# Experts, projection and solution of a two-block transformer in one block, with two norms behind the experts as one step

## The reference

```python
# first block, end: product-key experts, then the norm that closes the block
h2 = rmsnorm(x, g_ffn)
x = x + peer_ffn(h2, w_peer_q, sub_keys, u_tab, v_tab)
x = rmsnorm(x, g_final)
# second block, start: norm, gated delta rule in both directions
h = rmsnorm_2(x, norm_mix[0])
x = x + gated_deltanet_bidir(h, ...)   # projection, conv, decays, triangular solution, w_out
x = x + squared_relu_mlp(rmsnorm_2(x, norm_mlp[0]), w1, w2)
# then a dilated window attention with its own norm, a second mlp, a last norm
def rmsnorm(x, g):
    return x * rsqrt(mean(x * x) + 1e-6) * g
```

## Time and profile before

| | us |
|---|---|
| time, median of 3 runs | 1988.34 (1986.02 to 1992.40) |
| profiled execution, device time | 1990.63 |
| profiled execution, span of the trace | 1988.5 |
| TensorE busy in the span | 1880.9 (95%) |
| VectorE busy | 1289.9 (65%) |
| ScalarE busy | 898.8 (45%) |
| mean granted TensorE clock | 0.972 of 2.4 GHz |

### The profile page before, as it was taken

One profiled execution on the slowest core, in us unless ns is written; L12 is line 12 of the kernel. 1 busy time (PEld: TensorE's weight loads), 2 busy tenths in 40 slices (PEclk: granted clock), 3 DMA queues, 4 the chain that ended last, 5 costly groups with the idle time before them and its releaser, 6 DMA issues. The chain is left out here.

```text
span 1988.5 us, 31375 instructions
## 1 busy us (share of the span) xinstructions
PE 1880.9 (95%) x13035; PEld 1741.9 (88%) x13035; DVE 1289.9 (65%) x2034; ACT 898.8 (45%) x1161; POOL 18.1 (1%) x24
## 2 busy tenths in 40 slices
PE   7999998999999999999999969888899999999997
PEld 7998897899999999888888859778799889789985
DVE  5656874798788888655555557885466455446633
ACT  6457532343443433444444446666255343435532
POOL 0000000000000000000000000000000001000000
PEclk9999999999999999999999979987899999999999
DMA  6443354444444444455555533310254456525443
GB/s 225 171 172 132 123 191 152 146 174 171 157 146 153 147 152 146 179 209 190 191 191 196 196 127 129 126 44 23 77 178 169 186 198 210 131 74 191 177 183 117
DMA packets 44741, 310.66 MB, mean 156 GB/s; under 512 B 5166, under 2 KB 5678, under 8 KB 8144
## 3 DMA queue, kind: packets, MB, share of 16 engines
q1 hardware_dynamic: 42576, 303.58, 42.3%
q0 software_dynamic: 1472, 4.86, 1.5%
q10 hardware_dynamic: 576, 0.55, 0.1%
HBM read 306.84 MB, written 2.13 MB: 155 GB/s over the span
## 5 line engine op out<-in xcount | busy, mean ns | idle before, releaser
L310 DVE TENSOR_TENSOR s_ring_lo<-s_ring,s_w_hi 128x2048 fp32r<-128x2048 f32 x236 | 540.6, 2291 | 253.1 <-ACT s_w_hi L304 248.6
L304 ACT ACTIVATE s_w_hi<-s_ring 128x2048 fp32r<-128x2048 f32 x235 | 448.1, 1907 | 157.3 <-PE bank L347 77.9
L347 PE MATMUL bank<-s_hT_hi,s_w_hi 128*128 128x256 f32 x2016 | 292.8, 288 | 4.3 <-PEq L455 2.4
L347 PE MATMUL bank<-s_hT_hi,s_ring_lo 128*128 128x256 f32 x2016 | 285.4, 285 | 1.0 <-DVE s_ring_lo L310 0.8
L347 PEld LDWEIGHTS bank<-s_hT_hi,s_w_hi 128*128 128x128 f32 x2016 | 263.2, 194 | 9.5 <-issue 8.1
L347 PEld LDWEIGHTS bank<-s_hT_hi,s_ring_lo 128*128 128x128 f32 x2016 | 262.2, 194 | 1.8 <-DVE s_ring_lo L310 1.8
L1544 PE MATMUL bank<-s_w_hi,s_hT_lo 128*128 128x512 f32 x1024 | 242.6, 389 | 0.3 <-issue 0.3
L1544 PEld LDWEIGHTS bank<-s_w_hi,s_hT_lo 128*128 128x128 f32 x1024 | 192.1, 188 | 40.3 <-issue 0.4
L347 PE MATMUL bank<-s_hT_lo,s_w_hi 128*128 128x256 f32 x1056 | 152.2, 288 | 0.0
L347 PEld LDWEIGHTS bank<-s_hT_lo,s_w_hi 128*128 128x128 f32 x1056 | 140.3, 197 | 0.0
L347 PE MATMUL bank<-s_x_r,s_w_hi 128*128 128x256 f32 x960 | 134.8, 283 | 0.0
(11 more groups left out here) (413 smaller groups left out, 2413.6 us busy)
## 6 DMA issues: line engine op xcount, KB each, us to landing
s_ring<-weights SPq DMA_DIRECT2D x282, 1024.0 KB, 4.8
s_arena<-bias_by_distance POOLq DMA_DIRECT2D x12, 384.0 KB, 7.4
s_arena<-mem SPq DMA_DIRECT2D x1, 1024.0 KB, 6.0
s_x<-x SPq DMA_DIRECT2D x1, 1024.0 KB, 13.6
x_away<-s_x SPq DMA_DIRECT2D x1, 1024.0 KB, 4.8
s_arena<-sub_keys SPq DMA_DIRECT2D x1, 1024.0 KB, 6.9
s_arena<-x_away SPq DMA_DIRECT2D x1, 1024.0 KB, 6.8
out<-s_x SPq DMA_DIRECT2D x1, 1024.0 KB, 4.0
```

The lines of the kernel that those rows point to most:

```text
L304: act.activation(k.w_hi[:, u % 2, :], k.ring[:, u % RING, :], ACT.Copy).then_inc(k.hi_ready, 1)
L310: dve.tensor_tensor(k.ring_lo[:, u % RING, :], k.ring[:, u % RING, :], plain(k.w_hi[:, u % 2, :]), ALU.subtract).then_inc(k.lo_ready, 1)
L347: last = pe.matmul(out[:, nb * S:(nb + 1) * S], w[:, c, nb * P:(nb + 1) * P], h[:, c, :], start=(n == 0 and c == 0), stop=(n == 2 and c == 7))
```

## The change

- The first two blocks' semaphores are allocated by hand and cleared ahead of the norm before the experts, instead of those of the experts and the projection being cleared behind these.
- `peer`, `gdn_project` and `back_half` become stages of one block; the block ends between experts, the two norms, projection and solution are gone, and the SyncE stream runs through.
- The two norms behind the experts become one `DoubleSeam`. With s = 1/(mean(x^2)+eps), w = x g, t = 1/(mean(w^2) s + eps), the normed x is w sqrt(s) and the input of the projection is w sqrt(s t). The last unit of the experts is ordered bank by bank, each bank reports, and VectorE adds it and multiplies by g; ScalarE squares both. The turn is a product with a diagonal of sqrt(s t). g_final is loaded during the downs. The normed x is written later, beside unit 0.
- Next weights: the halves of the projection's first unit are made ahead of the additions; a Sqrt on one column is issued before the squares.
- Solution: the two pairs of banks of the decays are renamed so that head 0 can start ahead of the projection's last results, with waits of its own for each.
- `gdn_out`: the addition of unit n comes ahead of `split_lo` of unit n+2. Last group of a half in the mlp: high and low half are waited for one by one.

The diff, cut; pure changes of indentation are left out.

```diff
+class DoubleSeam(Seam):
+    def __init__(self, k, gcol, banks):
+        Seam.__init__(self, k, gcol, banks)
+        k.doubles += 1
+        self.g_rows, self.w, self.junk = carve(k, 2 * D, D), carve(k, 4 * D, TT, D), carve(k, 6 * D, TT, 2, 512)
+        ...
+    def squares(self, act, dh, tt):
+        at, n = slice(dh * 512, (dh + 1) * 512), 2 * dh + tt
+        act.wait_ge(self.k.x_added, self.at + n + 1)
+        act.activation(self.junk[:, tt, dh, :], self.k.x[:, tt, at], ACT.Square,
+                       accum_out=self.x_sums[:, n:n + 1]).then_inc(self.x_squared, 1)
+        act.wait_ge(self.weighed, n + 1)
+        act.wait_ge(self.x_squared, n + 1)
+        act.activation(self.junk[:, tt, dh, :], self.w[:, tt, at], ACT.Square,
+                       accum_out=self.w_sums[:, n:n + 1]).then_inc(self.w_squared, 1)
+    def factors(self, dve, own):
+        ...
+        dve.wait_ge(self.x_squared, 4)
+        own.up(dve.tensor_tensor(m, self.x_sums[:, 0:2], self.x_sums[:, 2:4], ALU.add))
+        own.up(dve.tensor_scalar(m, m, 1.0 / D, EPS, ALU.mult, ALU.add))
+        own.up(dve.reciprocal(both[:, 0:2], m))
+        dve.wait_ge(self.w_squared, 4)
+        own.up(dve.tensor_tensor(t, self.w_sums[:, 0:2], self.w_sums[:, 2:4], ALU.add))
+        own.up(dve.tensor_tensor(t, t, both[:, 0:2], ALU.mult))
+        own.up(dve.tensor_scalar(t, t, 1.0 / D, EPS, ALU.mult, ALU.add))
+        own.up(dve.reciprocal(self.product[:, 0:2], t))
+        dve.tensor_tensor(both[:, 2:4], self.product[:, 0:2], both[:, 0:2], ALU.mult).then_inc(self.factor_ready, 1)
+        dve.wait_ge(self.root_ready, 1)
+        for tt in range(TT):
+            last = dve.tensor_scalar(self.one[:, tt, :], self.k.ident, self.roots[:, 2 + tt:3 + tt], None, ALU.mult)
+        last.then_inc(self.one_ready, 1)
+    def take_root(self, act):
+        act.wait_ge(self.factor_ready, 1)
+        act.activation(self.roots, self.both, ACT.Sqrt).then_inc(self.root_ready, 1)
+    def normed(self, dve):
+        for tt in range(TT):
+            dve.tensor_scalar(self.k.x[:, tt, :], self.w[:, tt, :], self.roots[:, tt:tt + 1], None, ALU.mult)
+    def turn(self, pe, j):
+        pe.wait_ge(self.one_ready, 1)
+        for c in range(2):
+            for tt in range(TT):
+                last = pe.matmul(self.k.ps[self.banks[j]][:, c * S + tt * P:c * S + (tt + 1) * P],
+                                 self.w[:, tt, (2 * j + c) * P:(2 * j + c + 1) * P], self.one[:, tt, :],
+                                 start=True, stop=True)
+        last.then_inc(self.k.x_turned, 1)
+    def unit(self, pe, u, out):
+        for j in range(2):
+            self.turn(pe, j)
+        Seam.unit(self, pe, u, out, 2)
 ...
 # peer, SyncE
                     sp.dma_start(x_back.rearrange("p t d -> p (t d)"), k.x_away).then_inc(k.x_here, 16)
+            if u == F + PAIRS + RING + 6:
+                sp.dma_start(seam.g_rows, k.args["g_final"].partition_broadcast(P)).then_inc(k.g_here, 16)
 ...
 # peer, TensorE, in down(d, i)
+            if d == PAIRS - 1:
+                split_ready(k, pe, v, 0, turn=i * 4)
+                split_ready(k, pe, v, 2, turn=i * 4)
+                for dh in range(2):
+                    for tt in range(TT):
+                        for n, (g, w) in enumerate(((g_hi, w_hi), (g_lo, w_hi), (g_hi, w_lo))):
+                            for b in range(2):
+                                last = pe.matmul(ps[4 + 2 * tt + dh][:, :], g[:, b, tt * P:(tt + 1) * P],
+                                                 w[:, b, dh * 512:(dh + 1) * 512], start=False,
+                                                 stop=(n == 2 and b == 1))
+                        if (dh, tt) != (1, 1):
+                            last.then_inc(bank_done, 1)
+                last.then_inc(k.unit_done, 1)
+                return
 ...
 # peer, ScalarE, at its end
+        split_hi(k, act, U["gdn_qkv"])
+        act.activation(seam.spare, k.ident[:, 0:1], ACT.Sqrt)
+        for dh in range(2):
+            for tt in range(TT):
+                seam.squares(act, dh, tt)
 ...
 # peer, VectorE, at its end
-            dve.wait_ge(k.unit_done, F + 128)
+        split_lo(k, dve, U["gdn_qkv"])
         dve.wait_ge(k.x_here, 16)
-            for tt in range(TT):
-                for dh in range(2):
+        dve.wait_ge(k.g_here, 16)
+        for dh in range(2):
+            for tt in range(TT):
                 at = slice(dh * 512, (dh + 1) * 512)
-                    own.up(dve.tensor_tensor(k.x[:, tt, at], x_back[:, tt, at], ps[4 + 2 * tt + dh][:, :], ALU.add))
+                if (dh, tt) == (1, 1):
+                    dve.wait_ge(k.unit_done, F + 128)
+                else:
+                    dve.wait_ge(bank_done, 2 * dh + tt + 1)
+                dve.tensor_tensor(k.x[:, tt, at], x_back[:, tt, at], ps[4 + 2 * tt + dh][:, :], ALU.add)\
+                   .then_inc(k.x_added, 1)
+                dve.wait_ge(k.x_added, seam.at + 2 * dh + tt + 1)
+                dve.tensor_tensor(seam.w[:, tt, at], k.x[:, tt, at], seam.g_rows[:, at], ALU.mult)\
+                   .then_inc(seam.weighed, 1)
 ...
 # gdn_project, at the start of each engine
+        sp.wait_ge(k.unit_done, U["gdn_qkv"])
+        pool.wait_ge(k.unit_done, U["gdn_qkv"])
+            if n == 0:
+                seam.unit(pe, U["gdn_qkv"], ps[0])
+                return
+        seam.take_root(act)
+        for j in range(4):
+            seam.round_hi(act, j)
         split_hi(k, act, U["gdn_qkv"] + 1)
+        seam.factors(dve, own)
+        for j in range(4):
+            seam.round_lo(dve, j)
+        seam.normed(dve)
         split_lo(k, dve, U["gdn_qkv"] + 1)
 ...
 # gdn_solve
-    RI, RA, KK, NAT = ps[0:2], ps[2:4], ps[4:6], ps[6:8]
+    RI, RA, KK, NAT = (ps[1], ps[0]), ps[2:4], ps[4:6], ps[6:8]
         def keys(h):
+            pe.wait_ge(g.scaled, min(6 + h, H))
         for h in range(H):
-            if h >= 2:
+            if h == 0:
+                pe.wait_ge(g.evacuated, H + H // 2)
+            elif h == 1:
+                pe.wait_ge(g.first_z_out, 1)
+            else:
                 pe.wait_ge(decays_ready, h - 1)
 ...
         for n in range(4):
-            if n < 2:
-                split_lo(k, dve, U["gdn_out"] + n + 2)
             dve.wait_ge(k.unit_done, U["gdn_out"] + n + 1)
             for tt in range(TT):
                 xs = k.x[:, tt, n * S:(n + 1) * S]
                 last = dve.tensor_tensor(xs, xs, ps[(4 + 2 * n + tt) % 8][:, 0:S], ALU.add)
             last.then_inc(k.x_added, 1)
+            if n < 2:
+                split_lo(k, dve, U["gdn_out"] + n + 2)
 ...
 # mlp, last group of a half
-                    split_ready(k, pe, u + 1, 0)
-                    split_ready(k, pe, u + 1, 2)
                     if pair == 0:
                         pe.wait_ge(mid_ready, B + 4 * (q + 1))
                     for tt in range(TT):
                         for n in range(3):
+                            if tt == 0:
+                                split_ready(k, pe, u + 1, n)
                             last = product(n, tt)
 ...
 # program
     merge(k)
+    k.nc.clear_and_free_semaphores(k.first_sems)
+    k.nc.clear_and_free_semaphores(k.second_sems)
     normalise(k, k.x, col(k, "g_ffn", KC), k.hT, 0)
     k.whole_units += FIRST["peer"] - FIRST["peer_q"]
-    peer(k)
-    ...
-    normalise_rows(k, k.x, k.args["g_final"], k.x)
-    normalise(k, k.x, col(k, "g_a", KC), None, 0, split=(k.hT_hi, k.hT_lo, FIRST["gdn_qkv"]))
-    ...
-    gdn_project(k)
     back_half(k)
```

1044 lines of the change are left out of this document (530 added, 514 removed).

## The result

| | before | after |
|---|---|---|
| median (lowest to highest), 4 runs each | 1990.37 (1986.02 to 1992.91) | 1966.11 (1962.44 to 1969.88) |
| ratio, 95% interval | | 0.9880 [0.9864, 0.9896] |
| profiled execution, its span | 1990.63, 1988.5 | 1967.95, 1966.2 |
| mean granted clock | 0.972 | 0.980 |

The changed kernel was run once more as an experiment (5 runs, median 1969.73, ratio 0.9897 [0.9878, 0.9916]); all nine executions have the median 1967.95. The forecast was 1969.3 us with a range of 1963 to 1979. Of the kernel before, a fourth execution (1992.91) has come to the three that the prediction had, and its median is now 1990.37 and not 1988.34.

What follows compares the result with a forecast made beforehand. TensorE, busy 95% of the span, was taken as the bound, time being won where it waits or runs at the lower clock. 7.6 + 0.7 + 7.6 + 3.2 = 19.1 us off the median of 1988.3 gave 1969.3 us, range 1963 to 1979.

Steps and rivals of the forecast that it cites:

- the ends of the terms: Lowest and highest gains of the four parts, together 10.7 to 21 us, so 1967 to 1978 us.
- the sign of being wrong: Whole kernel: among the signs against the prediction was a total gain outside 15 to 22 us.
- Part 1: Seam behind the experts, through projection unit 0: shorter norm chain, earlier first turn; gain 7.0 to 8.1, taken 7.6 us.
- Part 2: Projection to solution: ScalarE starts sooner, TensorE may fall to the lower clock; gain -0.2 to 1.9, taken 0.7 us.
- Part 3: Output projection: addition first removes two TensorE waits and the lower clock behind them; 7.6 us, or 4.4 without the clock.
- Part 4: Feed-forward, last group of each half: weight halves awaited one by one; gain 3.2 us, 2.5 to 3.3.
- Lower clock at the seams: Rival: TensorE stays at 1.2 GHz through unit 0, solution gains nothing, output projection only 4.4 us; 1976.7 us, chance 0.15.
- The new chain is no shorter: Rival, seam behind the experts: hand-overs between steps cost more, losing 5 to 8 us; 1974 to 1977 us, chance 0.08.
- Given back: Rival: time won at the seam and output projection returns as waits for weights; about 1984 us, chance 0.05.
- Slower: Rival: more TensorE time at the lower clock between 1160 and 1440 us eats the gain; up to 1995 us, chance 0.02.
- GpSimd holds VectorE up: Rival, seam: three memsets, 3.82 us in all, block VectorE's additions and multiplications; 1973.1 us at full blocking, chance 0.06.

Runs made afterwards that it cites:

- e6: Changed kernel with 28 extra products into an unread bank, filling TensorE's hole ahead of the first turn; median 1964.82 us, ratio 0.9874.
- e9: Changed kernel with the last expert unit multiplied part by part again, all four banks ending together, additions waiting for its end; 1965.69 us, one run.
- e4: Kernel before with two edits alone: addition ahead of the split in the output projection, split waits of the last feed-forward groups; median 1981.19 us, ratio 0.9951.
- e0: Changed kernel run again without any edit, for the scatter; median 1969.73 us, ratio 0.9897 to the kernel before.
- e1: Changed kernel with the output projection's order undone: VectorE splits unit n+2 before adding unit n to x; median 1970.08 us, ratio 0.9903.
- e5: Changed kernel with VectorE's low half of the projection's first unit moved behind the norm's factors; median 1966.12 us, ratio 0.9883.
- e10: Changed kernel with the low half behind the factors, 22 filling products in the hole and 10 ahead of the solution's head 2; median 1965.09 us, ratio 0.9872.
- e11: Kernel of e5 with GpSimd's three memsets held until the seam's diagonal matrices are ready; median 1965.03 us, ratio 0.9869 to the kernel before.
- e2: Changed kernel with the last product group of each feed-forward half waiting for both weight halves at its start again; median 1972.06 us, ratio 0.9909.

## Why the prediction was right, point by point

**The sum.** 19.1 us were forecast, the spans differ by 22.3 and the medians by 24.3 (22.4 with all nine executions). The time lies in the range, on its lower side, with all four terms of the right sign. The gain is another matter: it lies above the 21 us that the ends of the terms give, and outside the 15 to 22 us that the prediction itself named as the sign of being wrong. That the time came so near the forecast is partly luck, as the forecast was taken from a median of before that a further execution raised by 2.0 us. The lower end of the range was also put at 1963 where its own working (1967 less 2) gives 1965; the measured 1966.11 lies above both. By the stages of the two profiles the four parts gave 7.59, 1.3, 8.69 and 3.95 us; 2.3 us more are in the last of the points below, and 1.6 us were lost before the experts.

**Part 1, forecast 7.6 us.** From the experts' end to unit 1: 27.19 us before, 19.60 after, 7.59 less. Two misses of 0.2 us cancel out. The first turn came 7.14 us behind the experts' end, forecast 7.35: the first addition starts 1.18 us ahead of the end (assumed 1.1), the eight steps take 5.37 instead of 5.8 us, since from a multiplication to the next addition it is 0.60 and not 0.72 us, and the last square ends 1.2 us behind them instead of 0.9. From there to the first turn it is 1.8 us as forecast, with the five small steps of the list (three more run under the last square). From the first turn to unit 1 it is 12.46 us, forecast 12.25; the clock rose within the 8 products behind the first turns, as placed (2.50 us, and 1.54 with the hole filled), and its whole price in unit 0 is 2.1 to 2.3 us (e6). The order by banks was not priced by itself in the prediction; it is 1.33 us (e9). Unit 1's halves were in time, as was the shift of the memsets and small loads.

**Part 2, forecast 0.7 us.** From the projection's end to the key sum it was 20.45 us before (20.40 in e4), and 19.15, 18.5 or 20.05 with the change, so 1.3 us less in the profile after, 1.9 in seven other traces and 0.4 in three. All lie in the range of -0.2 to 1.9; the 0.7 is a middle of two cases that both occur. The mechanism with its counter-mechanism was right, and whether TensorE falls to the lower clock in heads 2 and 3 decides between them: exponentials sooner than with the start held (by 1.4 us in the profile after, by 0.5 in e0), TensorE's wait of 2.5 us, and, where the lower clock came, ScalarE's wait of 1.43 us. Of the gain the held kernel keeps 1.4 us (19.03), so what removing the block end brought, and what the early start, is not split further by one profile.

**Part 3, forecast 7.6 us.** 7.78 in e4, 8.69 in the profile after (0.9 of it at the stage's start, where before and e4 still ran at the lower clock), and 6.33 when it is undone (e1). From start to start the two waits cost 4.7 us and not the 4.36 of the brackets; the clock's share, which I had put at 3.2, is 3.1 in the trace of before and 1.7 in e1.

**Part 4, forecast 3.2 us.** 3.95 in the profile, 3.75 in e4. The step that was mis-sized is the cost of the three waits, which I read as the idle time in brackets: from the start of one group to the start of the next the lost time is 1.15 and 2.81 us in the two layers, some tenths more per place than the brackets have. Undone in the changed kernel they cost 6.4 us, because one wait was 2.28 us in that trace, with a load that landed later, and the lower clock came behind it.

**Not in the sum.** 1.7 us between the key sum and the output projection, and 0.6 us between the gates and the projection's end (89.9 and 89.3 us). In the trace of before the third unit of z ran at the lower clock, in that of after at the higher, and the same six groups of eight take 8.18 (1333.10 to 1341.28) and 5.83 us (1324.85 to 1330.68):

```profile
1333.10 2.06 PE L347 MATMUL bank<-s_hT_hi,s_w_hi 128*128 128x256 f32 x8
...
1349.00 1.76 PE L2263 MATMUL bank<-s_arena 32*32 32x32 f32 x45 [4.55 <-ACT s_arena L2450]
```

```profile
1324.85 1.19 PE L347 MATMUL bank<-s_hT_hi,s_w_hi 128*128 128x256 f32 x8
...
1338.41 1.76 PE L2375 MATMUL bank<-s_arena 32*32 32x32 f32 x45 [2.10 <-ACT s_arena L2562]
```

The first fence is of before, the second of after. The second row of each is the solution's step at level 5 that waits for ScalarE's work on this unit: it comes 7.7 us behind the unit's last product in both. So the late unit shows as 13.18 instead of 10.74 us between level 5 and level 6; 0.3 us more come ahead of level 5, and 1.0 us is given back behind level 6. The prediction dealt with the clock only at the places that the change touches.

**The rivals.** *Lower clock at the seams* did not come (1976.7): unit 0 went to the higher clock where forecast. *The new chain is no shorter* fell: 0.03 us between VectorE's steps. *Given back* fell: TensorE's waits for weight halves at L347 are 1.6 and 1.5 us in all, 1.6 and 1.4 before. *Slower* fell: the clock did move the time, but the other way (mean 0.972 before, 0.980 after). *GpSimd holds VectorE up* came to nothing in the changed kernel, and the experiments show why. The memsets ran from 1163.37 to 1167.19 beside six big steps of VectorE that kept their 0.68 to 0.69 us. The sort of step that a memset does hold, a tensor_scalar over data in SBUF, came first at 1168.07, 0.9 us after the memsets' end. Moved earlier it was held to the end of the memset, twice (e5, e10), and freed with the memset moved (e11). The Trainium skill, GPSIMD Engine Reference, Specifications, names two sorts of VectorE instructions that contend with GpSimd: those in a two-port mode and those with two SBUF inputs. The first sort is borne out at 0.51 us, if L478 is one; the Trainium skill, VectorE: DVE Perf Modes, Mode 2×_2P, says that a tensor_scalar on data in SBUF can use both read ports for its one tensor, and no run here shows which mode L478 had. The second is not, beside a memset: L1901 has two SBUF inputs and takes 0.69 us beside the memset of 2.67 us and also without it (0.69 in e11).

## What to carry to other kernels

The factors of one or two norms can be put into the products that turn the rows, so that no pass over the data stands between the factors and the turn; what is paid is twice the records for the turn (1.7 us here, half of the turns at the lower clock), and the chain in front of it became 6.8 us shorter. That is the gain of the whole new seam: 1.33 us of it are the order by banks (e9), and how the rest divides between the single norm, the earlier load of g_final and the earlier root table, no run shows. On an engine's queue, the step that another engine waits for goes ahead of the one that has slack, and a wait for two things becomes two waits where they are used: these two orders alone gave 9.4 us of 24.3. A small change in a kernel with holes of several us should be judged by the stage it touches, over repeated profiles: a hole costs its length and, behind it, between nothing and 2.3 us through the lower clock (e1, e2, e6), and the lower clock comes and goes in stages that were not touched, even between two profiles of one kernel (e0).
